# Pairs of weight slots, the place of the residual write, and one buffer for inner rows, in a kernel of a hybrid backbone layer

## What is computed

```python
def expert_choice_ffn(u, w_router, w_gate, w_up, w_down):
    cap = EC_FACTOR * l // N_EXPERTS                 # 64 of the 512 tokens, 16 of the 128
    probs = jax.nn.softmax((u @ w_router), axis=-1)
    aff, idx = lax.top_k(jnp.swapaxes(probs, 1, 2), cap)
    xs = u[bidx, idx]
    hid = jax.nn.silu(einsum('becd,edf->becf', xs, w_gate)) * einsum('becd,edf->becf', xs, w_up)
    ys = einsum('becf,efd->becd', hid, w_down) * aff[..., None]
    return jnp.zeros_like(u).at[bidx, idx].add(ys)

x = layer_norm(ALPHA * x + g1 * mixed, ln1_g, ln1_b)
u = layer_norm(x) * (1.0 + sc2) + sh2
x = layer_norm(ALPHA * x + g2 * expert_choice_ffn(u, ...), ln2_g, ln2_b)
```

## Time and profile before

| | us |
|---|---|
| median of 3 runs | 1450.13 |
| lowest and highest | 1448.92, 1451.91 |
| profiled execution, whole time | 1453.37 |
| its span, first to last instruction | 1451.5 |
| PE busy | 1356.6 (93%) |
| VectorE (DVE) busy | 614.1 (42%) |
| ScalarE (ACT) busy | 229.3 (16%) |
| GpSimd (POOL) busy | 75.0 (5%) |
| mean granted TensorE clock | 0.976 of full |
| read from HBM, written | 280.36 MB, 17.30 MB |

### The profile page before, as it was taken

One profiled execution on the slowest core, in us unless ns is written; L12 is line 12 of the kernel. 1 busy time (PEld: TensorE's weight loads), 2 busy tenths in 40 slices (PEclk: granted clock), 3 DMA queues, 4 the chain that ended last, 5 costly groups with the idle time before them and its releaser, 6 DMA issues.

```text
span 1451.5 us, 24005 instructions
## 1 busy us (share of the span) xinstructions
PE 1356.6 (93%) x10632; PEld 758.9 (52%) x10632; DVE 614.1 (42%) x1342; ACT 229.3 (16%) x464; POOL 75.0 (5%) x62
## 2 busy tenths in 40 slices
PE   6999999998999999999999984999999999999991
PEld 2455554656989985666765441434434444334430
DVE  6222237636777762543423774422224222222205
ACT  4311122223333332110110022000000000000000
POOL 0000000000000000000000001011111111111100
PEclk9999999998999999999999996999999999999996
DMA  9822212401000000330132056999999999999974
GB/s 387 356 109 106 93 41 108 173 9 67 3 2 2 3 16 7 168 149 26 58 130 88 37 225 271 389 395 397 401 388 397 396 382 401 401 401 399 415 295 156
DMA packets 31971, 299.21 MB, mean 206 GB/s; under 512 B 3419, under 2 KB 7643, under 8 KB 15484
## 3 DMA queue, kind: packets, MB, share of 16 engines
q1 hardware_dynamic: 20876, 270.93, 46.3%
q0 software_dynamic: 7584, 16.78, 4.6%
q10 hardware_dynamic: 3408, 9.96, 1.7%
HBM read 280.36 MB, written 17.30 MB: 205 GB/s over the span
## 4 chain that ended last, share of the span: by engine, by line
PE 57%; DMA 8%; DVE 4%; issue 1%; ACT 0%; SPq 0%; DVEq 0%; ACTq 0%; POOLq 0%
PE bank L592 56%; DMA ring<-w_e_down_dram 5%; DMA front<-w_e_down_dram 3%; DVE hbuf L1972 1%; PE bank L1034 1%; DVE hbuf L2158 0%; DVE stats L2156 0%; DVE front L1741 0%; DMA y_dram<-front,misc 0%; DMA front<-u_dram,misc 0%; DMA hbuf<-y_dram 0%; DVE misc L2023 0%; PE bank L529 0%; DVE misc L2021 0%; DVE front L2024 0%
## 5 line engine op out<-in xcount | busy, mean ns | idle before, releaser
L592 PE MATMUL bank<-front,ring 128*128 128x128 f32 (+3 forms) x1416 | 402.7, 443 | 3.9 <-ACT front L1265 1.1
L592 PE MATMUL bank<-ring,front 128*32 128x256 f32 (+3 forms) x2640 | 352.0, 459 | 4.4 <-issue 2.2
L592 PEld LDWEIGHTS bank<-front,ring 128*128 128x128 f32 (+1 forms) x1416 | 223.5, 189 | 183.5 <-issue 163.8
L592 PE MATMUL bank<-front 128*32 128x256 f32 (+4 forms) x3152 | 298.4, 359 | 7.1 <-DVE front L1741 3.4
L592 PEld LDWEIGHTS bank<-ring,front 128*32 128x32 f32 (+3 forms) x2640 | 152.1, 126 | 198.0 <-issue 159.9
L592 PEld LDWEIGHTS bank<-front 128*32 128x32 f32 (+3 forms) x3152 | 177.1, 139 | 116.5 <-issue 81.4
L592 PE MATMUL bank<-hbuf,front 128*32 128x256 f32 (+3 forms) x736 | 109.5, 433 | 0.0
L2089 DVE STREAM_TRANSPOSE front<-front 32x256 f32<-32x256 f32 x180 | 78.2, 434 | 25.3 <-DMA front<-u_dram,misc 20.1
L592 PEld LDWEIGHTS bank<-hbuf,front 128*32 128x32 f32 (+2 forms) x736 | 57.6, 140 | 47.9 <-issue 31.5
L1530 DVE SCALAR_TENSOR_TENSOR front<-bank,pk,front 128x511 f32<-128x511 f32 x64 | 32.2, 545 | 99.4 <-ACT front L1131 98.8
L1741 DVE COPY_PREDICATED front<-ck,bank 128x256 f32<-128x256 uint32 (+1 forms) x120 | 52.7, 443 | 32.5 <-PE bank L592 22.1
(11 more groups left out here) (290 smaller groups left out, 1002.9 us busy)
## 6 DMA issues: line engine op xcount, KB each, us to landing
ring<-w_e_down_dram SPq DMA_DIRECT2D x18, 2048.0 KB, 27.6
ring<-w_e_gate_dram SPq DMA_DIRECT2D x16, 2048.0 KB, 26.5
ring<-w_e_up_dram SPq DMA_DIRECT2D x16, 2048.0 KB, 24.0
front<-w_e_gate_dram SPq DMA_DIRECT2D x12, 2048.0 KB, 26.7
front<-w_e_up_dram SPq DMA_DIRECT2D x12, 2048.0 KB, 27.2
ring<-w_in_dram SPq DMA_DIRECT2D x11, 2048.0 KB, 8.0
front<-w_e_down_dram SPq DMA_DIRECT2D x11, 2048.0 KB, 29.0
ring<-w_mod_dram SPq DMA_DIRECT2D x10, 2048.0 KB, 12.8
```

The costliest lines, as they stand in the source:

```text
L592: return pe.matmul(out, lhsT, rhs, start=(k == 0), stop=(k == n - 1))
```

## The change

Three edits:

1. `SLOT_PAIRS` gives matrices 0, 4, 8, ... the slots 0 and 2, and matrices 1, 5, 9, ... the slots 1 and 3. Before, it was 0 and 1, and 2 and 3.
2. GpSimd issues the five writes of y_dram and waits until they have landed, and only then waits for `gather_row` and issues `gather(0)`.
3. For expert 15 alone the turned inner rows go to xsT[0] instead of hdT, and the copy doesn't wait for the down product of expert 14.

```diff
-SLOT_PAIRS = ((0, 1), (2, 3), (6, 7), (4, 5))
+SLOT_PAIRS = ((0, 2), (1, 3), (6, 7), (4, 5))
...
-                sample(m, bank[7], hdT).then_inc(sem("down_s_mm"), 1)
+                sample(m, bank[7], hdT if e < E - 1 else xsT[0]).then_inc(sem("down_s_mm"), 1)
...
             def inner_sample(e):
                 act.wait_ge(sem("hid_tr"), e + 1)
-                if e:
+                if 0 < e < E - 1:
                     act.wait_ge(sem("down_s_mm"), e)
-                A(hdT.rearrange("p (h j) s -> p h j s", h=2), by_block(6, 0, 64, 4), ACT.Copy).then_inc(sem("hidT_s"), 1)
+                dst = hdT if e < E - 1 else xsT[0]
+                A(dst.rearrange("p (h j) s -> p h j s", h=2), by_block(6, 0, 64, 4), ACT.Copy).then_inc(sem("hidT_s"), 1)
...
-            pool.wait_ge(sem("gather_row"), 1)
-            gather(0)
             for t in range(NT):
                 pool.wait_ge(sem("scaled"), t + 1)
                 pool.dma_start(y_dram[P * t:P * t + P, :], h[:, t, :]).then_inc(sem("y_start"), 16)
             pool.wait_ge(sem("y_start"), 16 * NT)
+            pool.wait_ge(sem("gather_row"), 1)
+            gather(0)
             pool.wait_ge(sem("lane_rows"), 2)
```

## The result

The changed kernel took 1458.67 us (median of 4 runs, 1458.47 to 1461.16), the kernel before 1450.20 on the same chip (4 runs, 1448.92 to 1451.91). The ratio is 1.0052, with an interval of 1.0036 to 1.0067, that is 5.2 to 9.7 us slower. The direction was forecast, the size was not: 1453.2 was expected, and 1458.67 lies above the upper end of the range, 1457.5. The profiled execution took 1458.48 us.

What follows compares the result with a forecast made beforehand. Expert-loop weight loads and TensorE were almost level, behind a gather chain without slack. PE's 6.8 us delay less recovered waits and clock gave +2.1 to +4.2, middle +3.1: 1453.2 us, range 1449.0 to 1457.5.

Steps and rivals of the forecast that it cites:

- Part 1 at nothing: First expert loads: the new slot pairs alone were worth 0, with 1 us as the bound.
- The y_dram writes: Ahead of the first gather: the writes were to land at 887.8, bounds 885 and 889.7.
- the forecast's 0.4 us of wait: First gather: issued at 888.1 instead of 887.74, as it waits for the y_dram writes.
- The gather beside the load: Before the expert loop: the first gather beside matrix 6 takes 10.6 us, not 4.14, starting PE 6.8 us later.
- The rival in which the gather passes the load: First gather lands 4.1 us after issue despite matrix 6, total 1445.4; 13%.
- The head start: Expert loop: weights arrive 2.1 us later, PE 6.8 us later, so loads gain 4.7 us against PE's waits.
- The give-back: Expert loop: 4.0 us of weight waits, 1.7 of low clock and 0.1 of part 3 could be recovered.
- two signs that the prediction named: Expert loop: PE's waits for w_e_down fall to 2 us or less, and the mid-loop low clock goes.
- The reasoning about the median: Unprofiled runs: if the profile's 3.24 us excess is waits, the median gives back only 2.6, costing +4.2.
- the middle that I took: Whole time: +3.1 us, the middle of +2.1 and +4.2, giving 1453.2.
- Part 3 at 0.1 us: Last expert: ScalarE's inner copy runs some 7 us earlier, but VectorE's bank 7 read still holds PE; gain about 0.1 us.
- The loss in full: Expert loop: unprofiled runs hardly wait for weights, so the whole 6.8 us late start stays, 1456.9; 15%.

Runs made afterwards that it cites:

- slots_only: The kernel before with only the new slot pairs: 1451.64 us, ratio 1.0003 to the kernel before.
- slots_tail: The kernel before with the new slot pairs and expert 15's own buffer, gather still ahead of the y_dram writes: 1452.09 us, ratio 1.0000.
- after_light: The changed kernel with an eighth of the expert weight loads left out from matrix 7 on: 1453.09 us, ratio 1.0008 to the kernel before.
- yfirst_only: The kernel before with only the y_dram writes put ahead of the first gather: 1459.35 us, ratio 1.0052.
- four like it: Profiles of the unchanged kernel before again, and of it with new slot pairs, expert 15's buffer, or both: matrix 7 landed 51.7 to 52.3 us after PE's start.
- before_copy: The kernel before, unchanged, run again for a second profile: 1452.41 us, ratio 1.0001.
- the light loads: The kernel before with an eighth of the expert weight loads left out from matrix 7 on: 1445.74 us, ratio 0.9951.
- the four others that gather first: Second profile of the unchanged kernel before, and it with new slot pairs, expert 15's buffer, or both: loops of 519.3 to 520.5 us.
- the three profiles of the kernel after: The changed kernel, unaltered, profiled in three sets: 673.49 to 673.73 us from SP's first gate load to the end.
- the five from before to slots_tail: Two profiles of the kernel before, and it with new slot pairs, expert 15's buffer, or both: 667.72 to 670.27 us from SP's first gate load.
- the first comparison: The changed kernel against the kernel before, four runs each: 1458.67 against 1450.20 us, ratio 1.0052.
- the two others: The unaltered changed kernel against the kernel before in two later sets: 1456.15 us, ratio 1.0020, and 1456.61 us, ratio 1.0039.
- the three comparisons: The changed kernel against the kernel before in three sets: ratios 1.0052, 1.0020 and 1.0039, mean 1.0037.
- the second set: The changed kernel, unaltered, against the kernel before, beside both with lighter loads: 1456.15 against 1451.91 us, ratio 1.0020.
- after_third: The changed kernel, unaltered, a third time against the kernel before: 1456.61 us, ratio 1.0039.
- hold_again: The changed kernel with SP issuing matrix 6 only after the first gather has landed, second time: 1449.63 us, ratio 0.9979 to the kernel before.
- the held load: The changed kernel with matrix 6 issued only after the first gather landed: 1450.78 us, ratio 0.9992, then 1449.63 us, ratio 0.9979, to the kernel before.
- the exchanged slots: The kernel before with new slot pairs, expert 15's buffer and matrix 6's two slots exchanged: 1450.10 us, ratio 0.9981.

## Why the prediction was off, step by step

**Part 1 at nothing: right.** slots_only and slots_tail show 0 within 0.14%.

**The y_dram writes: right within the bounds.** Forecast to land at 887.8, with matrix 6 and the gather released at 888.1; they landed at 888.1, and SP issued at 888.19. That the two agree so closely is luck: this execution began 1.8 us late, and counted from SP's first gate load the writes landed after 103.2 us and not after 104.7, 1.5 us early. So the forecast's 0.4 us of wait was 0, as gather_row was ready later than the writes.

**The gather beside the load: right.** 10.6 us forecast from the second gather of before, 9.9 to 10.2 measured in the four profiles of the kernel after and after_light, 9.94 in yfirst_only. That makes PE 5.9 us late by the gather (10.04 - 4.14), where 6.8 was forecast. The rival in which the gather passes the load fell.

**The head start: wrong, and this is the step that failed.** "From there the queue is full again and every load keeps this distance" gave weights 2.1 us late against PE's 6.8, and 4.7 us to set against the waits. To compare the pair of profiles, the 1.8 us by which the second began late must come off. The second half of matrix 4 landed at 917.1 + 12.2 = 929.3, that is 927.5 on the clock of before, 1.2 us ahead of the 928.7 forecast. Matrix 5 landed at 927.6 + 14.2 = 941.8, or 940.0: 3.0 us later than the 937.0 of before and not 2.1. Matrix 7 landed at 939.0 + 15.9 = 954.9, or 953.1: 3.8 us later than 949.3. With PE 5.9 us later, the head start was 2.9 us at the second load and 2.1 at the third. 13.3 us from first issue to landing was near enough for an idle queue (12.5 for matrix 4); for matrix 5 it was 14.6, as it met a queue in which matrix 4 was still under way. And even the 2.1 us rest on the one profile whose loads lagged 1.5 to 2.1 us more than in four like it, as the table shows.

**The give-back: wrong with it.** The sum took 5.8 us from one execution, 4.0 of waits, 1.7 of low clock and 0.1 of part 3, as what could be given back. The waits are there in most executions: 3.7 us in before_copy, and the light loads are worth 6.2 us. But only a part of them vanishes when PE starts late. The wait for w_e_down in `front`, 2.7 us in before and 0.9 to 2.2 in the four others that gather first, is in none of the three profiles of the kernel after. The wait for w_e_down in `ring` stays (1.6 to 1.7 us, where before_copy waits 1.6), and so do short ones for other weights: 2.4 to 2.6 us in all, against 3.2 to 4.5 in the five from before to slots_tail. The low clock of 1.7 us went too, but not by the change: before_copy, which starts early, has a loop without that loss as well, and so have all other profiles. So two signs that the prediction named, waits for w_e_down of 2 us or less and no low clock in the middle of the loop, came true without the gain that they stood for. The row of before_copy for the stretch in which before lost it, columns as above:

```profile
1260.00:1285.00 25.00, 23.27 (x230) 9.92 (x226) 4.56 (x10) 1.19 (x2) 3.11 (x2) 1.00 1.01 405
```

The same 25 us stand at a clock of 0.93 in before. The forecast of +3.1 was 6.8 us of late start less 3.7 given back. By the traces the late start is 6.3 to 6.4 us (5.9 to 6.1 of the gather, the rest of low clock), a little less than forecast, and what came back is 0.4 to 3.2, the most of it only against the one unusual profile. That gives +3.2 to +6.0. The +8.5 of the first comparison is more than the late start itself; by 2 us it stays unexplained, and it did not come again (+4.2 and +4.3 by the medians of the two others). The reasoning about the median (2.6 to give back, +4.2) was sounder in direction than the middle that I took, but it too used up the whole head start against the waits.

**Part 3 at 0.1 us: right.** The copy runs a whole product early now, but the gap stays. Three engines at the last down product of the kernel after (timeline):

```profile
1407.34 0.60 ACT L1338 ACTIVATE front<-bank 128x512 f32<-128x512 f32 x1 [14.11 <-PE bank L1036]
...
1414.37 0.75 DVE L2121 SCALAR_TENSOR_TENSOR front<-bank,misc 128x512 f32<-128x512 f32 x1 [6.61 <-PE bank L592]
...
1415.22 2.37 PE L592 MATMUL bank<-ring,front 128*64 128x512 f32 x10 [0.90 <-issue]
```

PE waits the same 0.90 us, and starts when VectorE has read bank 7 (1414.37 + 0.75 = 1415.12). The profile puts it down to "issue" and does not name VectorE, as I had said it would; that it is VectorE rests on these two times.

**The rivals.** The loss in full, 1456.9 at 15%, was the nearest in number to the first comparison. In mechanism it is near too, but not for its reason: it decided where the runs hardly wait for weights, and they do wait. The mean of the three comparisons, +5.4, lies between it and the forecast. By the medians of the second set 7.35 - 4.2 = 3.1 us came back. So the traces say that 0.4 to 3.2 us come back of 6.4, one set says that half of the late start may, and the first comparison says none. What is open: how much an average run gives back between 0 and 3 us, by what the landing of the loads differs between executions of one program, and whether the chips of the sets differ. No kernel was profiled often enough to tell.

## What to carry to other kernels

When one event releases a bulk load and a small transfer that the critical engine waits for, let the load wait for the small one: here one extra wait on SP took a gather from 10 to 3.9 us and the kernel from 1456.61 to 1449.63 us (after_third and hold_again), and the loads of the loop were none the later for it. A late start is repaid by the waits that come after it only as far as the loads keep their old times, and loads that are issued when PE frees a slot do not: here they moved with PE, and a head start of 3.5 us and more at the first load was at most 1.5 us two loads later, against the four usual profiles. A give-back that is read from one profiled execution should be held against a second one before it is counted.

## What was not expected of the hardware

A gather of 80 rows (0.33 MB) takes 3.8 to 4.3 us on idle DMA engines and 9.2 to 10.6 beside a load of 2.1 or of 4.2 MB; between these two sizes of the neighbour it hardly differs, its presence is what costs. While both are in flight, from 894 to 898, the engines are at a share of 1.04 and move 311 GB/s, against 393 in the stretch of the loop shown above.

Profiles of one program differ long before the loop: SP issues the first gate matrix at 783.10 in before and 781.15 in before_copy, and at 784.91, 784.49 and 782.63 in the three profiles of the kernel after. Counted from there, these three agree within 0.24 us to the end. In the loop, the kernel before took 521.95 us once and 519.7 once, and the first time it had a stretch at the lower clock that the second had not. The best two kernels, the held load and the exchanged slots, are 2 to 3 us faster than before by one comparison each (0.9979 and 0.9981), about what a run can tell; the first comparison of the held load, 0.9992, does not show it.
